# Local attention of a hybrid encoder on one NeuronCore: values as the stationary operand, probabilities divided on ScalarE

## What is computed

```python
def windowed_gqa(q, k, v, sink):            # blocks of 128 queries, 2 or 3 blocks of keys
    s = einsum(q, k) / sqrt(HEAD_DIM)
    s = where(mask, s, NEG)
    m = maximum(max(s), sink)
    p = exp(s - m)
    denom = sum(p) + exp(sink - m)
    return einsum(p / denom, v)              # S x 512
y_att = rms_norm(windowed_gqa(...), att_g)   # over the 512 of a token
y = concatenate([y_att, y_mlstm]) @ w_out
x = layer_norm(ALPHA * x + y, ...)
```

## Time and profile before

| | |
|---|---|
| median of 3 runs | 2233.62 us (2233.3 to 2236.38) |
| profiled execution | 2236.14 us |
| its span (first to last instruction) | 2234.6 us |
| mean granted TensorE clock | 0.98 of full speed |
| TensorE busy | 2109.9 us, 94% |
| VectorE busy | 1330.3 us, 60% |
| ScalarE busy | 996.6 us, 45% |
| attention groups of layer 0 | about 80 to 283 us |
| recurrence groups and first half of the output projection, layer 0 | about 284 to 387 us |
| first and last score matmul of layer 1's groups | 1164 to 1350 us |

### The profile page before, as it was taken

The page is one execution under the profiler, slowest core; times in us unless marked ns, Lnnn a source line. Parts: engine busy times, 40 slices in busy tenths (PEclk is TensorE's granted clock), DMA queues, the critical chain, the costliest instruction groups (busy, mean ns, idle before and its releaser), DMA issues.

```text
span 2234.6 us, 31576 instructions
## 1 busy us (share of the span) xinstructions
PE 2109.9 (94%) x11392; PEld 1698.4 (76%) x11392; DVE 1330.3 (60%) x2057; ACT 996.6 (45%) x1656; POOL 227.8 (10%) x268
## 2 busy tenths in 40 slices
PE   7899999999999899999798999999999989999997
PEld 7778867888887577777577887788887867777774
DVE  3785477831454756566878646783325476665566
ACT  3554565232422354555235547533333135555553
POOL 0000023000000311000200001300000032200004
PEclk9999999999998899999899999999999999999999
DMA  4164112221102699999511112023120059999996
GB/s 153 57 198 147 39 76 96 95 94 57 57 29 100 232 369 376 385 377 347 197 58 38 39 39 95 20 115 115 74 76 10 38 215 371 372 378 377 374 383 222
DMA packets 78534, 384.88 MB, mean 172 GB/s; under 512 B 10473, under 2 KB 11865, under 8 KB 43609
## 3 DMA queue, kind: packets, MB, share of 16 engines
q1 hardware_dynamic: 55264, 327.31, 38.8%
q0 software_dynamic: 10096, 30.38, 3.9%
q10 hardware_dynamic: 13064, 25.75, 3.1%
HBM read 352.27 MB, written 46.07 MB: 178 GB/s over the span
## 4 chain that ended last, share of the span: by engine, by line
PE 73%; DVE 14%; ACT 7%; issue 2%; DMA 2%; POOL 1%; DVEq 0%; ACTq 0%; POOLq 0%; SPq 0%
PE bank L2201 30%; PE bank L2712 10%; PE bank L2686 8%; PE bank L2676 7%; PE bank L2413 5%; PE bank L2444 2%; PE bank L2523 2%; DVE weight_slots_parts L1437 2%; PE bank L2222 1%; PE bank L2652 1%; ACT scratch L1059 1%; DVE scratch L1599 1%; PE bank L2567 1%; PE bank L2583 1%; PE bank L2606 1%
## 5 line engine op out<-in xcount | busy, mean ns | idle before, releaser
L1907 DVE TENSOR_TENSOR weight_slots_parts<-weight_slots,mixer_region_parts 128x2048 fp32r<-128x2048 f32 x140 | 322.9, 2327 | 85.5 <-ACT mixer_region_parts L1261 85.4
L2201 PE MATMUL bank<-weight_slots_parts,x_transposed_parts 128*128 128x256 f32 (+1 forms) x1248 | 299.1, 334 | 7.0 <-DVE mixed L1559 4.2
L1261 ACT ACTIVATE mixer_region_parts<-weight_slots 128x2048 fp32r<-128x2048 f32 x140 | 260.9, 1909 | 23.2 <-ACT x_transposed L1336 18.1
L2201 PE MATMUL bank<-x_transposed_parts,weight_slots_parts 128*128 128x512 f32 (+1 forms) x1024 | 262.7, 343 | 6.9 <-DVE mixer_region L1551 3.7
L1437 DVE TENSOR_TENSOR weight_slots_parts<-weight_slots,weight_slots_parts 128x2048 fp32r<-128x2048 f32 x58 | 132.9, 2292 | 193.5 <-ACT weight_slots_parts L950 192.8
L2712 PE MATMUL bank<-weight_slots,x_transposed 128*128 128x512 f32 x560 | 248.0, 596 | 0.0
L2201 PEld LDWEIGHTS bank<-weight_slots_parts,x_transposed_parts 128*128 128x128 f32 x1248 | 210.7, 193 | 26.2 <-DVE mixed L1559 5.0
L2686 PE MATMUL bank<-mixer_region_parts,x_transposed_parts 128*128 128x256 f32 x1120 | 207.7, 283 | 0.7 <-DVE weight_slots_parts L1907 0.6
L2201 PEld LDWEIGHTS bank<-x_transposed_parts,weight_slots_parts 128*128 128x128 f32 x1024 | 180.0, 193 | 28.7 <-DVE mixer_region L1551 4.5
L2676 PE MATMUL bank<-mixer_region_parts,x_transposed_parts 128*128 128x512 f32 x560 | 193.9, 418 | 4.6 <-DVE x_transposed_parts L1912 4.6
L2712 PEld LDWEIGHTS bank<-weight_slots,x_transposed 128*128 128x128 f32 x560 | 104.2, 191 | 118.8 <-issue 103.2
(11 more groups left out here) (319 smaller groups left out, 3590.3 us busy)
## 6 DMA issues: line engine op xcount, KB each, us to landing
weight_slots<-in_w_gate SPq DMA_DIRECT2D x70, 1024.0 KB, 7.4
weight_slots<-in_w_up SPq DMA_DIRECT2D x70, 1024.0 KB, 7.2
weight_slots<-in_w_down SPq DMA_DIRECT2D x70, 1024.0 KB
weight_slots<-in_w_in SPq DMA_DIRECT2D x20, 1024.0 KB, 5.2
slots_y<-x_transposed ACTq DMA_DIRECT2D x66, 256.0 KB, 7.3
...
```

Of the source, the lines that this page charges most:

```text
L1261: nc.scalar.activation(hi, raw, ACT.Copy).then_inc(moe.high_ready, 1)
L1907: v.tensor_tensor(lo, raw, hi.bitcast(F32), ALU.subtract).then_inc(moe.low_ready, 1)
L2201: ins = pe.matmul(ps, lhs[i](k), rhs[j](k), start=k == 0 and a == 0, stop=k == KD - 1 and a == 2)
```

## The change

Three things change in the attention loop, and what lies behind it follows.

- The sums and reciprocals of group i are made right behind its exponentials (`denominators(i)`, VectorE waits for `p_ready` there, before its stream tiles). ScalarE waits for them (`p_scaled`) and multiplies the probabilities of the four heads by the reciprocals, in place. `p_ready` now counts two signals a group, and TensorE waits for the second before it turns the probabilities.
- The turned probabilities are packed: nb tiles of four transposes each, where there were four tiles of nb.
- The values are the weights (64 columns) and the turned probabilities move (256 columns, two heads of one key head), into partitions 0 to 63 or 64 to 127 for key head 0 or 1. The output of a group stands turned, width on the partitions, and ScalarE copies it to `y` (256 columns).

Behind it: no `attention_scaled`, no turns ("yt", c, 0). ScalarE squares the turned output of a chunk (512 columns), VectorE sums over the four (`sum_squares`, a strided TENSOR_REDUCE), and TensorE sums over the partitions by a product with a column of ones (("rs", 0) and ("rs", 1)). ScalarE makes 1/rms of it at the end of g = 0, with ALPHA folded in. High and low parts come from `y` in SBUF (`high_y`, `low_y_attention`). The gain is multiplied into the first half of w_out as wo0 and wo1 are split: four ScalarE operations of 512 columns for one of 2048, four VectorE operations for one. The rows of w_out and the gains are laid out for it ahead of the kernel. The first half is added as tile * (1/rms) + x, the second as ALPHA * x + tile.

The diff, cut to its core:

```diff
-    for j in range(GRP):
-        add(("pt", i - 1, j), (4, 5))
+    for b in range(keys_of(GROUP_ORDER[i - 1][0])[1]):
+        add(("pt", i - 1, b), (4, 5))
...
+    add(("rs", 0), (4, 5))
...
-        for c in YT_BEHIND[s] if g == 0 else ():
-            add(("yt", c, 0), (4, 5, 6, 7))
+    if g == 0:
+        add(("rs", 1), (7,))
...
+                elif name in ("wo0", "wo1"):
+                    act.wait_ge(unit_loaded[slot_of(name)], loads_of(name))
+                    act.wait_ge(rows_loaded, 64 * now[0] + 64)
+                    hi, raw = half_hi(name, GRP), half_raw(name, GRP)
+                    for j in range(GRP - 1):
+                        nc.scalar.activation(hi[:, j, :], raw[:, j, :], ACT.Copy, scale=lane_gain[:, j:j + 1])
+                    nc.scalar.activation(hi[:, GRP - 1, :], raw[:, GRP - 1, :], ACT.Copy,
+                                         scale=lane_gain[:, GRP - 1:GRP]).then_inc(w_hi, 1)
...
-                act.wait_ge(cv_used, 16 * l + 16)
-                step(nc.scalar.activation(esc[:, :], y[:, c, 0:ATT], ACT.Square, accum_out=st[:, 20 + c:21 + c]))
-
+                if c < NC - 1:
+                    tile_filled(act, ("sc", 2 * c + 1, GRP - 1))
+                    out = qT[:, :, c * P:(c + 1) * P]
+                else:
+                    act.wait_ge(cv_used, 16 * l + 16)
+                    out = esc[:, :].rearrange("p (j t) -> p j t", j=GRP)
+                nc.scalar.activation(out, y_turned[:, c, 0:GRP, :], ACT.Square).then_inc(turned, 1)
+                own(turned)
+
+            def attention_rstd(part, c0, n):
+                key = ("rs", part)
+                tile_filled(act, key)
+                step(nc.scalar.activation(st[:, 20 + c0:20 + c0 + n], bank_of(key)[:, 0:n], ACT.Ln, bias=eps_att,
+                                          scale=ALPHA * ALPHA / ATT))
+                nc.scalar.activation(st[:, 20 + c0:20 + c0 + n], st[:, 20 + c0:20 + c0 + n], ACT.Exp,
+                                     scale=-0.5).then_inc(drain_sem(key), 1)
+                tile_drained(act, key)
+
+            def high_y(c):
+                tile_filled(act, STREAM[-1])
+                nc.scalar.activation(x_hi[:, 0:GRP, c * P:(c + 1) * P], y_turned[:, c, 0:GRP, :], ACT.Copy).then_inc(turned, 1)
+                own(turned)
...
-                    n = keys_of(GROUP_ORDER[i - 1][0])[1] * P
-                    for j in range(GRP):
-                        key = ("pt", i - 1, j)
-                        tile_filled(act, key)
-                        nc.scalar.activation(ptb[:, j, 0:n], bank_of(key)[:, 0:n], ACT.Copy).then_inc(drain_sem(key), 1)
-                        tile_drained(act, key)
+                    for b in range(keys_of(GROUP_ORDER[i - 1][0])[1]):
+                        drain_copy(("pt", i - 1, b), ptb[:, 512 * b:512 * b + 512], 512)
...
+                if i < 12:
+                    act.wait_ge(p_scaled, 12 * l + i + 1)
+                    for j in range(GRP):
+                        ins = nc.scalar.activation(probs[:, j, 0:nk], probs[:, j, 0:nk], ACT.Copy, scale=st[:, 110 + j:111 + j])
+                    ins.then_inc(p_ready, 1)
+                    own(p_ready)
+                if i:
+                    c, jp = GROUP_ORDER[i - 1]
+                    drain_copy(("pv", i - 1), y[:, c, 256 * jp:256 * jp + 256], 256)
 
                 if 7 <= i < 12:
                     square_of(i - 7)
-                if i == 11:
-                    rstd(st[:, 20:25], st[:, 20:25], 5, 1.0 / ATT, eps_rms).then_inc(att_rs, 1)
-                    own(att_rs)
...
-                            rstd(st[:, 25:26], st[:, 25:26], 1, 1.0 / ATT, eps_rms).then_inc(att_rs, 1)
-                            own(att_rs)
                         if g == 0:
                             for c in ((), (0, 1), (2, 3, 4), (5,))[sc]:
-                                high_x(("yt", c, 0), c, 0)
+                                high_y(c)
                 if g == 0:
                     stream_tile(STREAM[-1])
+                    attention_rstd(0, 0, NC - 1)
+                    attention_rstd(1, NC - 1, 1)
...
+            def low_y_attention(c):
+                dve.wait_ge(turned, len(TURNED) * now[0] + TURNED[("yt", c, 0)] + 1)
+                v.tensor_tensor(y_lo[:, c, 0:GRP, :], y_turned[:, c, 0:GRP, :], x_hi_at(c, 0).bitcast(F32),
+                                ALU.subtract).then_inc(att_parts, 1)
+                own(att_parts)
...
+                elif name in ("wo0", "wo1"):
+                    lo, hi, raw = half_lo(name, GRP), half_hi(name, GRP).bitcast(F32), half_raw(name, GRP)
+                    for j in range(GRP):
+                        ins = v.scalar_tensor_tensor(out=lo[:, j, :], in0=raw[:, j, :], scalar=lane_gain[:, j:j + 1], in1=hi[:, j, :],
+                                                     op0=ALU.mult, op1=ALU.subtract)
+                    ins.then_inc(w_lo, 1)
...
-            def attention_scaled(c):
-                v.scalar_tensor_tensor(out=y[:, c, 0:ATT], in0=y[:, c, 0:ATT], scalar=st[:, 20 + c:21 + c],
-                                       in1=gmix[:, 0:ATT], op0=ALU.mult, op1=ALU.mult).then_inc(y_att, 1)
-                own(y_att)
+            def sum_squares(c):
+                dve.wait_ge(turned, len(TURNED) * now[0] + TURNED[("squares", c)] + 1)
+                sq = qT[:, :, c * P:(c + 1) * P] if c < NC - 1 else esc[:, :].rearrange("p (j t) -> p j t", j=GRP)
+                v.tensor_reduce(sums_at(c), sq.rearrange("p j t -> p t j"), AX.X, ALU.add).then_inc(att_parts, 1)
+                own(att_parts)
+
+            def denominators(i):
+                dve.wait_ge(p_ready, 24 * l + 2 * i + 1)
+                step(v.tensor_tensor(st[:, 110:114], st[:, 8:12], st[:, 12:16], ALU.add))
+                v.reciprocal(st[:, 110:114], st[:, 110:114]).then_inc(p_scaled, 1)
+                own(p_scaled)
 
             for i in range(13):
                 w = slot_tiles(i)
-                if i:
-
-                    dve.wait_ge(p_ready, 12 * l + i)
-                    ro = 110 + 4 * ((i - 1) % 2)
-                    step(v.tensor_tensor(st[:, ro:ro + 4], st[:, 8:12], st[:, 12:16], ALU.add))
-                    step(v.reciprocal(st[:, ro:ro + 4], st[:, ro:ro + 4]))
                 if i < 12:
                     c, jp = GROUP_ORDER[i]
                     _, nb, m0 = keys_of(c)
                     nk = nb * P
                     if i:
 
-                        tile_filled(dve, ("pt", i - 1, 3))
+                        tile_filled(dve, ("pt", i - 1, keys_of(GROUP_ORDER[i - 1][0])[1] - 1))
...
+                if i < 12:
+                    denominators(i)
                 if w and i:
                     stream_tile(w[0])
-                if i == 12:
-                    dve.wait_ge(att_rs, 2 * l + 1)
-                    for c in range(NC - 1):
-                        attention_scaled(c)
-                if i:
-                    c, jp = GROUP_ORDER[i - 1]
-                    key = ("pv", i - 1)
-                    tile_filled(dve, key)
-                    step_ = v.tensor_tensor(y[:, c, 0:ATT].rearrange("p (n j d) -> p n j d", n=NKV, j=GRP)[:, :, 2 * jp:2 * jp + 2, :],
-                                            bank_of(key)[:, 0:256].rearrange("p (j n d) -> p n j d", j=2, n=NKV),
-                                            st[:, ro:ro + 4].rearrange("p (j n) -> p n j", n=NKV).unsqueeze(3)
-                                            .broadcast_to([P, NKV, 2, HD]), ALU.mult)
-                    step_.then_inc(drain_sem(key), 1)
-                    tile_drained(dve, key)
+                if i >= 8:
+                    sum_squares(i - 8)
...
+            def attention_half(h, c):
+                key = ("wa", h, c)
+                tile_filled(dve, key)
+                xh = x[:, c, 512 * h:512 * h + 512]
+                v.scalar_tensor_tensor(out=xh, in0=bank_of(key)[:, :], scalar=st[:, 20 + c:21 + c], in1=xh,
+                                       op0=ALU.mult, op1=ALU.add).then_inc(drain_sem(key), 1)
...
-                v.tensor_tensor(xh, xh, bank_of(key)[:, :], ALU.add).then_inc(drain_sem(key), 1)
+                v.scalar_tensor_tensor(out=xh, in0=xh, scalar=ALPHA, in1=bank_of(key)[:, :],
+                                       op0=ALU.mult, op1=ALU.add).then_inc(drain_sem(key), 1)
...
-                def turn_probs(j):
+                def turn_probs():
                     c, _ = GROUP_ORDER[i - 1]
                     nb = keys_of(c)[1]
-                    key = ("pt", i - 1, j)
-                    ps = take(key)
-                    for k in range(nb):
-                        ins = pe.transpose(ps[:, k * P:(k + 1) * P], probs[:, j, k * P:(k + 1) * P], ident)
-                    done(ins, key)
+                    for b in range(nb):
+                        key = ("pt", i - 1, b)
+                        ps = take(key)
+                        for q in range(4):
+                            j, k = divmod(4 * b + q, nb)
```

(37 more changed lines are left out.)

60 lines of the change are left out of this document (37 added, 23 removed).

## The result

The kernel after took 2320.72 us (median of four runs, 2311.35 to 2321.51) against 2234.28 before: ratio 1.0385, interval 1.0365 to 1.0404. Slower, as forecast, but by 86 us where 41 were forecast, and above the range. The profiled execution is its fastest, 2311.35 us, so the traces have 74.3 us to account for (2308.9 - 2234.6).

The account below looks back on a forecast made before the run. Though TensorE was 94% busy, groups were taken as bound by masks, exponentials and turns across three engines. Terms 11.4 + 2.1 + 3.0 + 1.9 + 4.9 - 2.7 gave +20.6 a layer, +41.2 in all: 2274.8 us, range 2262 to 2286.

Parts of the forecast that it names:

- the tail: Last turns to first numerators: -2.7 us a layer from one wait gone, small products with ones lying beside.
- (a): Rival: TensorE stays the bound and the hand-offs hide; 17 to 26 us a layer gained, 2182 to 2200; chance 0.08.
- (b): Rival: link partly hidden, convolution groups pay, later ones win; +3 to +9 us a layer, 2240 to 2252; chance 0.17.
- (d): Rival: the walk finds chains that slack hides, and gains meet losses; 2230 to 2238 us; chance 0.05.
- Index 6, 7 and 8: Groups where value tiles wait for banks that ScalarE empties late: +2.1 at index 6, +3.0 for 7 and 8.
- rival (c): New stalls, at index 2, lower TensorE's clock; +6 us a layer, 2287; chance 0.13.
- The link's price: Division after the exponentials: VectorE's sums and inversion 0.4 us, then ScalarE's four scalings 1.8 or 2.25 us a group.
- index 9: Drain behind a split and low parts comes 1.3 us later, a sum of squares goes ahead: +1.9 us.
- index 10 and 11: Dearer wo0 split and low part, +2.75, then a gate tile's SiLU behind the scalings: in all +4.9 us.
- Sum of squares: At index 9, VectorE's sum goes ahead of the drain, priced at 0.6 us.
- Output weight: wo0's split and low part each become four operations ahead of index 11's masks: +2.75 us.
- Value product: Values as weights: the sum took nothing saved; the other bound, overlapping halves, gave 0.6 to 1.0 us a group.

Follow-up runs that it names:

- no division: Kernel after without the division of the probabilities: no sums, reciprocals or scalings; 2270.7 us, ratio 1.0173, with one extra expert block in layer 0.
- stalls filled: Kernel after plus 12 unread filler matmuls in each of groups 6 to 11: 2302.1 us; a second run also filled index 2 and 3: 2305.0 us.
- squares on TensorE: Kernel after with VectorE's sums of squares left to TensorE, four products with a column of ones a block instead of one; 2311.5 us, ratio 1.0349.
- plain wo: Kernel after without the norm's gains, both halves of the output weight split without them; 2305.0 us, ratio 1.0316.
- factors early: Kernel after with ScalarE making the norm's factors earlier behind the groups, not behind everything; 2319.8 us, ratio 1.0377.
- packing alone: Kernel before with only the packed turns of the probabilities; 2229.25 us against 2231.05, ratio 0.9988.

## Why the prediction was right in direction and half the size

**Where the 33 us went that the traces show beyond the 41.2.** The groups took 24.4 more than forecast in the two layers, of which 9.0 are the clock and 15.4 the division's link and the work beside it; the tail took 10.6 more, the stretch behind it 4.9; the experts and the rest gave 6.8 back. Another 12 us of the measured 86 have no trace.

**The mechanism held.** VectorE idles 27.8 us ahead of the sums in the groups of layer 0 (after, VectorE by shape),

```profile
L1637 DVE TENSOR_TENSOR small<-small 128x4 f32<-128x4 f32 x12 | 2.0, 164 | 27.8 <-ACT small L1096 27.8
```

The turns' waits are not shorter than before (16.1 for 10.5) and all but 0.2 stand at index 3 to 6, the masks of index 6 begin 13.7 us later counted from index 0 (11 forecast), the value tiles wait for the drain L1023. Rivals (a), (b) and (d) needed the link to hide. It costs 33.5 of 35.6 us (no division), some 4 of them by the clock.

**Index 6, 7 and 8 were sized about right, at the full clock.** Forecast 2.1, 1.5, 1.5. With stalls filled they are 1.9, 1.8 and 1.8. In the profiled execution two of them cost 2.3 and 1.5 more, because 48 records took 8.29 and 7.50 us for 6.0. This is rival (c), with a chance of 0.13, and it did happen beside the forecast and not instead of it: 4.1 and 4.9 us a layer here, near the 6 it was priced at. But I put it at index 2, where TensorE stands 3.9 and 3.2 us; there the clock fell to 0.58 and cost 0.4 us. The Trainium skill (TensorE: Matmul & The Clock Gate, HAM oscillation) has idle gaps between bursts lower the clock. The trace agrees, with a granted clock of 0.58 over 130 to 140 us and 1.00 with the stalls filled; that this costs time only where TensorE is on the chain is what filling them showed.

**The failed term is slack that wasn't there.** The link's price was nearly right: 0.4 and 1.8 or 2.25 us taken, 0.57 and 1.7 or 2.1 measured. What failed is how much of it I let hide behind other work. My terms hold about 20 us a layer of link (11.4 in index 0 to 5, 2.1, 3.0, 1.3 at index 9, 2.15 at 10 and 11). The run without division shows 33.5, or 29.4 when it is set against the run with filled stalls, which takes the clock out. Of the 9.4 between 20 and 29.4, 2.6 came at index 0 to 5 and 0.3 at index 6 to 8. The rest came behind: at index 9 I let 1.3 us through, 3.8 came; at index 10 and 11 2.15, and 6.3 came. In layer 1 these are 2.5 and 4.7, and index 0 to 8 have the more. So the walk for index 9 to 11, where I took the link to hide behind the split, the low parts and the gate tiles, is the step that was wrong most. There VectorE's drain of a gate tile (L1612) stands behind all of them, and TensorE waits 12.1 us for it in layer 0, 2.1 before. Once the first link is on the chain, the group is a loop through ScalarE's and VectorE's queues, and most of each further instruction ahead of the drain is paid. (The runs that leave out one thing don't add up at index 10 and 11, 6.3 of link, 3.0 of weights and 3.4 of squares against 8.4 in all: there they share waits.)

**Sum of squares.** 0.6 taken, once, at index 9. An instruction takes 1.03 us, and its place is index 10 and 11, 3.4 together (squares on TensorE; 3.1 in layer 1).

**Output weight.** 2.75 taken for index 10 and 11, 3.0 and 2.7 measured. The number was right by luck: the two differences that the prediction names, 0.65 on ScalarE and 0.71 on VectorE, make 1.36, and nothing in it says why 2.75 stands there. Why 3.0 came for so much less of added work isn't shown. And I counted wo0 alone. wo1's split, behind the groups, costs 1.7 and 2.6 us more (plain wo; the first is hardly clear of the spread), which the sum had at nothing.

**The tail.** -2.7 taken, though the one wait that it stands for is 2.2 in the row; +2.1 and +3.1 measured. This longer of the two waits for low parts did go, and one of 3.8 for L1068 took its place:

```profile
332.92 1.19 PE L2477 MATMUL bank<-weight_slots_parts,x_transposed_parts 128*128 128x512 f32 x2 [3.82 <-ACT small L1068]
```

The sum with ones took a bank (L2454) that the first output tile then waits for, and ScalarE empties it last. I had written that these small products lie beside: that step failed. With the factors early 2.3 us come back, and then the tail is as long as before (17.7 for 17.9 and 16.9), with TensorE waiting for decays and masks. So removing the 24 turns and the scalings gained nothing on balance.

**Value product.** I took the bound by which nothing is saved. The other was right: two blocks take 1.08 us for 1.75, and the records begin in pairs 0.007 us apart, so the column halves do overlap.

```profile
221.57 1.08 PE L2443 MATMUL bank<-scratch,mixer_region 128*64 128x256 f32 x8
```

That it changes no time here fits the runs, but no run leaves out this step alone. Without division TensorE has some 10 us a layer less to do, and the groups are still 2.1 and 1.3 us longer than before; index 7 and 8 take 15.6 us there and 15.4 with packing alone, which has the old value product.

**What stays open.** The median after is 9.4 us above the profiled execution. Groups as slow as those with the factors early (48 records in 8.60 us three times, groups 4 us longer in each layer, same code) would explain 8 of it, but those executions of the change have no trace, and the granted clock on record speaks against it: 0.959 in the profiled execution and 0.959, 0.959 and 0.957 in the other three, while with the factors early it goes from 0.960 at 2313 us to 0.954 at 2327. Per index, 0 to 5 came 0.15 to 0.8 us above forecast each; I didn't separate that.
